# A hybrid attention and mixture-of-experts block: the bias table on 128 partitions, one wait of TensorE dropped, roots warmed

## The reference

```python
h = layer_norm(concat([meta, x]), ln_in_g, ln_in_b)
qa, ka, va, qb, kb, vb, fb = split(h @ w_in)
o_a = sliding_sink_attention(qa, ka, va, sinks, rel_bias, pos, is_real)
o_b = forgetting_attention(qb, kb, vb, log_sigmoid(fb + b_f), key_valid)
h = layer_norm(DN_ALPHA * h + concat([o_a, o_b]) @ w_o, ln1_g, ln1_b)
ffn = hierarchical_moe(h, w_rg, b_rg, w_re, b_re, w_e_gate, w_e_up, w_e_down)
h = layer_norm(DN_ALPHA * h + ffn, ln2_g, ln2_b)
return h[:, N_META:]
```

## Time and profile before

| | |
|---|---|
| median of 3 runs | 2511.67 us (2507.01 to 2515.3) |
| the profiled execution | 2511.47 us |
| its span, first to last instruction | 2509.5 us |
| mean granted TensorE clock | 0.938 |
| TensorE matmul busy | 2196.5 us (88%) |
| VectorE busy | 1707.6 us (68%) |
| ScalarE busy | 1491.3 us (59%) |
| GpSimd busy | 330.4 us (13%) |

### The profile page before, as it was taken

How to read it: one execution, slowest core, us unless ns; L and a number is a source line. 1 busy time by engine, 2 the same in 40 slices (tenths; PEclk the granted TensorE clock), 3 DMA queues, 4 the chain that set the end, 5 groups by cost and what they waited for, 6 DMA issues and landing times. The chain is left out here.

```text
span 2509.5 us, 35865 instructions
## 1 busy us (share of the span) xinstructions
PE 2196.5 (88%) x11294; PEld 1790.3 (71%) x11294; DVE 1707.6 (68%) x3144; ACT 1491.3 (59%) x2261; POOL 330.4 (13%) x438
## 2 busy tenths in 40 slices
PE   7999899858859999999979994699999999999970
PEld 6778788645547777777858883587888888788860
DVE  5323231167668888888743334899999999899976
ACT  4323241256557767777633331587888888788856
POOL 0111111110000000000000000122222222222211
PEclk9999999969979999999989996799999999999985
DMA  6525352253252222220043331899787869999837
GB/s 196 175 101 152 126 178 87 76 133 88 64 132 60 66 68 66 68 68 9 8 165 144 142 125 51 294 374 328 240 261 238 281 228 340 325 301 303 270 79 285
DMA packets 213834, 420.06 MB, mean 167 GB/s; under 512 B 42920, under 2 KB 90104, under 8 KB 212824
## 3 DMA queue, kind: packets, MB, share of 16 engines
q1 hardware_dynamic: 180680, 314.15, 36.8%
q0 software_dynamic: 32016, 103.26, 14.3%
q10 hardware_dynamic: 1032, 1.31, 0.4%
HBM read 437.12 MB, written 86.39 MB: 209 GB/s over the span
## 5 line engine op out<-in xcount | busy, mean ns | idle before, releaser
L2348 DVE TENSOR_TENSOR moe_w_lo<-fetch_w_raw,moe_w_hi 128x1024 fp32r<-128x1024 f32 x376 | 435.2, 1217 | 9.4 <-ACT moe_w_hi L2277 9.1
L2277 ACT ACTIVATE moe_w_hi<-fetch_w_raw 128x1024 fp32r<-128x1024 f32 x376 | 368.5, 1053 | 63.9 <-PEq L92 32.5
L2402 PE MATMUL moe_ps_gu<-moe_w_hi,moe_xT_hi 128*128 128x512 f32 x736 | 293.8, 399 | 3.9 <-DVE moe_xT_lo L2359 3.9
L2404 PE MATMUL moe_ps_gu<-moe_w_hi,moe_xT_lo 128*128 128x512 f32 x736 | 289.3, 393 | 0.0
L2403 PE MATMUL moe_ps_gu<-moe_w_lo,moe_xT_hi 128*128 128x512 f32 x736 | 288.7, 392 | 0.0
L1355 ACT ACTIVATE fox_p_hi<-fox_ps_t 128x512 fp32r<-128x512 f32 (+4 forms) x352 | 181.2, 531 | 108.6 <-PE fox_ps_t L1495 107.8
L1422 DVE TENSOR_TENSOR fox_p_lo<-fox_ps_t,fox_p_hi 128x512 fp32r<-128x512 f32 (+4 forms) x352 | 211.0, 611 | 28.7 <-ACT fox_p_hi L1355 27.2
L1495 PE MATMUL fox_ps_t<-ident,fox_s 128*128 128x128 f32 (+1 forms) x1216 | 200.3, 280 | 29.3 <-ACT fox_s L1348 18.4
L2354 DVE TENSOR_TENSOR moe_d_lo<-fetch_d_raw,moe_d_hi 128x1024 fp32r<-128x1024 f32 x184 | 213.1, 1220 | 10.7 <-ACT moe_d_hi L2285 7.4
L1409 DVE CUSTOM_DVE_ANT_0 fox_s<-fox_ps_r,fox_ncum 128x512 f32<-128x512 f32 (+4 forms) x352 | 193.8, 569 | 21.0 <-PE fox_ps_r L1480 13.9
L1348 ACT ACTIVATE fox_s<-fox_s,fox_ntop 128x144 f32<-128x144 f32 (+5 forms) x192 | 173.4, 904 | 46.8 <-DVE fox_ntop L1417 46.3
(11 more groups left out here) (313 smaller groups left out, 4991.4 us busy)
## 6 DMA issues: line engine op xcount, KB each, us to landing
fetch_w_raw<-in_w_e_gate_dram SPq DMA_DIRECT2D x192, 512.0 KB
fetch_w_raw<-in_w_e_up_dram SPq DMA_DIRECT2D x192, 512.0 KB
fetch_d_raw<-in_w_e_down_dram SPq DMA_DIRECT2D x92, 1024.0 KB
proj_w_raw<-in_w_in_dram SPq DMA_DIRECT2D x24, 1024.0 KB, 5.2
proj_xt<-in_x_dram SPq DMA_DIRECT2D x16, 512.0 KB
h<-proj_hrow POOLq DMA_DIRECT2D x16, 512.0 KB, 3.4
win_q_raw<-qT SPq DMA_DIRECT2D x32, 256.0 KB, 4.0
mix_o<-o SPq DMA_DIRECT2D x16, 512.0 KB, 4.4
```

What stands on the lines that cost most here:

```text
L2277: nc.scalar.activation(w_hi[:, k], w_raw[:, k].rearrange("p j n -> p (j n)"), ACT.Copy).then_inc(gu_high, 1)
L2348: nc.vector.tensor_tensor(w_lo[:, k], w_raw[:, k].rearrange("p j n -> p (j n)"), w_hi[:, k].bitcast(F32), ALU.subtract).then_inc(gu_split, 1)
L2402: nc.tensor.matmul(out, xT_hi[:, slot, k], w_hi[:, k, cols], start=k == 0, stop=False)
L2404: done = nc.tensor.matmul(out, xT_lo[:, slot, k], w_hi[:, k, cols], start=False, stop=k == KT - 1)
```

## The change

The bias table is built on 128 partitions instead of 8, 16 partitions for each head. `relT` is loaded by eight loads (one for each head, its 32 values to 16 partitions), which stand behind the second group of chunk weights in SyncE's queue instead of behind the third input tile. The store of the table sends each partition's row 8 times, where it sent each of 8 rows 128 times. TensorE no longer waits at the end of the first quarter for the meta keys' sum; GpSimd still does. At the head of the projection, of the mixing stage and of the last stage ScalarE takes one root of the constant `eps` into a place that nothing reads.

```diff
--- before.py
+++ after.py
@@ -124,6 +124,7 @@
         std = m.sb("std", [P, 2])
         rstd = m.sb("rstd", [P, 2])
         eps = m.sb("eps", [P, 1])
+        root_first = m.sb("root_first", [P, 1])
         hT_hi = m.sb("hT_hi", [P, KT, SLOTS * P], F32R)
         hT_lo = m.sb("hT_lo", [P, KT, SLOTS * P], F32R)
         mT = m.sb("mT", [P, KT, 2 * META], F32R)
@@ -137,8 +138,8 @@
         logits = m.sb("logits", [P, 5, B_HEADS])
         meta_pair = m.sb("meta_pair", [P, 5, 2 * META])
         meta_k = m.sb("meta_k", [P, 5, META])
-        relT = m.sb("relT", [A_HEADS, N_BUCKETS])
-        table = m.sb("table", [A_HEADS, BIAS_TAB])
+        relT = m.sb("relT", [P, N_BUCKETS])
+        table = m.sb("table", [P, BIAS_TAB])
         forget, b_forget, one = gates["forget"], gates["b_forget"], gates["one"]
 
         ps_chunk = [m.ps(f"ps_chunk{i}", [P, SBT]) for i in range(2)]
@@ -288,12 +289,15 @@
             load_wv(3)
             load_x(2)
             sp.dma_start(b_forget[:], t["b_f"].rearrange("a h -> h a")).then_inc(table_in, 16)
-            with nc.allow_non_contiguous_dma(reason="a small table"):
-                sp.dma_start(relT[:], t["rel_bias"].rearrange("b h -> h b")).then_inc(table_in, 16)
             load_x(3)
             load_w(0)
             load_x(META_N)
             load_w(1)
+            copies = P // A_HEADS
+            with nc.allow_non_contiguous_dma(reason="a small table"):
+                for head in range(A_HEADS):
+                    sp.dma_start(relT[head * copies:(head + 1) * copies], row_broadcast(t["rel_bias"][:, head], copies)
+                                 ).then_inc(table_in, 16)
             for sb in range(SBS):
                 for i in range(QK):
                     if sb + 1 < SBS and i in NORM_AT:
@@ -421,6 +425,7 @@
                                          ACT.Copy).then_inc(chunk_out, 1)
 
             act.wait_ge(zero_ready, 1)
+            nc.scalar.activation(root_first[:], eps[:], ACT.Sqrt)
             norm(0)
             wv_high(0)
             wv_high(1)
@@ -455,8 +460,8 @@
                         gate_copy(sb)
                     if sb == 1 and i == 5:
                         act.wait_ge(table_done, 1)
-                        act.dma_start(t["table"][:, :, 0:BIAS_TAB],
-                                      table[:].unsqueeze(1).to_broadcast([A_HEADS, P, BIAS_TAB])).then_inc(table_stored, 16)
+                        act.dma_start(t["table"].rearrange("h r c -> (h r) c").rearrange("(p m) c -> p m c", p=P)[:, :, 0:BIAS_TAB],
+                                      table[:].unsqueeze(1).to_broadcast([P, A_HEADS, BIAS_TAB])).then_inc(table_stored, 16)
                     if ends_group(i):
                         G = group_of(sb, i) + 2
                         if G < GROUPS * SBS:
@@ -536,10 +541,10 @@
             weights_low(1)
             v_copy(3)
             v_copy(META_N)
-            dve.wait_ge(table_in, 32)
+            dve.wait_ge(table_in, 16 * (1 + A_HEADS))
             for a, b, bucket in bucket_runs(-BIAS_R0, BIAS_TAB - 1 - BIAS_R0):
                 done = nc.vector.tensor_copy(table[:, a + BIAS_R0:b + BIAS_R0 + 1],
-                                             relT[:, bucket:bucket + 1].to_broadcast([A_HEADS, b - a + 1]))
+                                             relT[:, bucket:bucket + 1].to_broadcast([P, b - a + 1]))
             done.then_inc(table_done, 1)
             for sb in range(SBS):
                 if sb > 0:
@@ -656,8 +661,6 @@
                         gate_turn(sb)
                     if sb + 1 < SBS and i in TURN_AT:
                         turn(tile_n(4 * (sb + 1) + TURN_AT[i]))
-                if sb == 0:
-                    pe.wait_ge(meta_k_ready, 1)
 
 
 def bucket_runs(lowest, highest):
```

## The result

| | before | changed |
|---|---|---|
| median of 6 runs | 2513.29 us | 2497.59 us |
| lowest and highest | 2507.01 to 2515.93 | 2491.25 to 2500.05 |
| the profiled execution | 2511.47 us | 2491.25 us |
| its span | 2509.5 us | 2489.6 us |
| first instruction of the window stage | 503.09 | 486.19 |

The ratio is 0.9937, with a 95% interval from 0.9926 to 0.9949: 15.8 us faster, 13 to 19. The projection became 16.90 us shorter. The two attention stages took 0.4 us longer, the mixing stage 0.2 us less; routing and experts took 2.7 us less, and the last stage 0.5. Nothing of the change is in the attention stages, in routing or in the experts. In the twelve profiles of this document that unchanged code varies by more: the attention stages take 763.7 to 771.8 us, routing and experts 907.9 to 914.3. So the profiled execution is a fortunate one, and the gain is that of the projection.

What follows compares the result with a forecast made beforehand. TensorE, busy for 88% of the span, was taken as the bound, so only its pauses and slow-clock time could be won: 2511.47 - 7.41 - 10.18 = 2493.9, as a median 2494 us, range 2489 to 2504.5.

Steps and rivals of the forecast that it cites:

- Part 1: End of the projection's first quarter: without TensorE's wait for the meta keys' sum, 12.34 us become 4.93, gaining 7.41 us.
- R3: Rival: TensorE stops at the first quarter's end for the turned tile's split instead, costing 5 us; 2499, chance 0.05.
- Part 2: Projection's second quarter: the table's store from 128 partitions no longer delays the input tile; six chunks gain 10.18 us.
- R1: Rival: the table's store still stalls the second quarter, from total traffic or packet width; 2504.3 us, chance 0.10.
- the bounds of 3.7 and 12.1: Store of the table: its duration in us at 64 packets an engine, at 58 or 189 ns each.
- Part 3: First quarter's load queue: eight small loads, 4,096 four-byte pieces at 13 ns, are through in time; cost 0.
- The budget of 33.7 us: First quarter: time from 41 to 74.7 for the small loads before TensorE is delayed; 132 ns for each packet.
- R4: Rival: the small loads hold the queue and delay the third weight group; slower, 2527 at 250 ns a packet, chance 0.02.
- R4's point of 221 ns a packet: Small loads: the packet time from which the delayed third weight group makes the kernel slower by over 0.3%.
- the row of 13 ns: Profile row used to price the small loads: 2,040 packets in 2 us at 84% of 16 engines.
- Part 4: Heads of projection, mixing and last stage: early roots move 1.28 us table loads off the first roots; taken as 0.
- R2: Rival: the three early roots shorten their stages as well, 3.8 us less; 2490.3 us, chance 0.05.

Runs made afterwards that it cites:

- the 16-neighbour kernel: The changed kernel with the table on 16 neighbouring partitions, two for each head, each sent 64 times by the store; 2496.98 us in its one run.

## Why the prediction was right

**The measured time.** 2494 was forecast, 2497.6 measured, within 2489 to 2504.5, and faster as forecast. Against the kernel before the gain is 15.7 us by the medians and 17.7 was forecast; the interval of the ratio holds both. The projection became 16.9 us shorter, where the sum has 17.6; the other 0.7 us is the late beginning of the first quarter's work. The rise of the kernel before's median from 2511.67 to 2513.29 is part of the run to run spread.

**Part 1, the wait.** Right in place and size: 4.93 us remain, no wait took its place (R3 falls), the clock stays at 1.00, and alone it gives 7.41 us at its place and 7.9 by the window stage. The clock's share, 2.45 us, is that of one profile; in the two others that keep the pause it is 1.85.

**Part 2, the store.** Right in size, 33.53 us for the six chunks, with the table alone 33.55; R1 falls. Its reason was half right. The step that failed is the sentence that the loads waited because eight partitions' worth of work sat on about eight engines: eight engines carry the same store without any stall if their partitions lie four apart, and 16 engines with the old slow packet do too. The duration I took, 6 us, came out at about 8, inside the bounds of 3.7 and 12.1, and the 16-neighbour kernel reached the upper bound and was still covered, as the bound said.

**Part 3, the small loads.** Cost 0, right. The price was wrong by more than a factor of three: 256 pieces on each engine were to take 3.4 us and passed from about 41 to 51, some 40 ns each. The step that failed is the choice of the row: its 2,040 packets carry 0.26 MB, some 128 bytes each, and pass at 84% of the engines; the pieces of four bytes pass while the engines are a fourth busy. What sets their pace is open. They pass as fast as they are issued, 430 in a microsecond, but the issue alone does not explain it: the last issue ended at 45.81, and from then until about 51 they still passed at that pace, 917 from 46 to 48. The price of an issue was wrong too, 0.4 us for a measured 1.2: the eight issues did not end before 43.63 but at 45.81, and the tile behind them went out 2.2 us late, inside its 14.6 us. The budget of 33.7 us was held by three times as many loads, whose pieces end between 71 and 72 against 74.7, and not by six times as many, which cost 29.1 us. But it was taken from the wrong path. R4's mechanism is right, the small loads hold the queue; its place is not. What TensorE felt was the input tile behind the loads, through ScalarE and the chunk's bank, and with three times as many loads that path had 1.3 us left, the table's about 3. The prediction had the tile among its numbers (14.6 us from issue to need) and priced only the weight group. R4's point of 221 ns a packet would by its own formula be reached with some five times as many loads (221 / 40, an estimate), not with the seventeen times that the row of 13 ns promised.

**Part 4, the roots.** Cost and gain 0, right: alone 1.0001, and R2's 0.9985 is excluded. The covers were those named: the shift's load in the projection (11.18) and the second tile's in the last stage (2441.26). In the last stage the shift's load, which releases VectorE at 2440.03, was a cover that the prediction had not named. No root was tried by itself, but the stages can be compared over the profiles: the mixing stage takes 268.4 to 269.8 us in the eight with its early root and 267.8 to 268.7 in the four without, the last stage 56.9 to 57.8 and 57.0 to 57.5. No gain of 1.28 us is to be seen in either. In the last stage the changed profile is 0.5 us shorter than the one before, more than the 0.3 us that was allowed, and this spread covers it.

**Open.** Why the two attention stages and the experts' stage vary by several us between executions of the same code was not studied. Nor was what sets the pace of the four-byte pieces, or why the same pause was followed by a longer stretch at 1.2 GHz in one profile than in two others.

## What to carry to other kernels

A stage that repeats itself gives its own measure: the same stretch in an undisturbed quarter gave the length of both mended stretches here to 0.1 us. A store that repeats a few rows out of neighbouring partitions was slow in every packet here; spread the rows over partitions that lie apart, or over all, before asking how many engines carry it. Price a load of many tiny pieces from a row with pieces as tiny, and not from any row of small packets. Then follow everything that stands behind it on its queue, the next tile as well as the next weights: going from 8 loads to 24 was free, and 48 cost 29 us.

## What the runs showed of the hardware that was not expected

- Loads of 512 pieces of four bytes take 1.19 us each to issue, 430 pieces a microsecond, while a fourth of the engines' time is used, and they go on passing at this pace for 5 us after the issue has ended; a load of 1,024 pieces of 1,024 bytes was issued in 0.43 us.
- A store's packet of 1,280 bytes takes 189 to 193 ns out of 8 or 16 neighbouring partitions, on 8 or 16 engines, and 63 ns out of 8 partitions four apart; all 128 together gave 72.
- TensorE started 1.55 us earlier, paused 2.40 us ten microseconds later, and ran the next 8 us at 1.2 GHz; started later, it paused 0.34 us there and kept 2.4 GHz. The earlier start ended 2.9 us behind.
